# Plain fp32 q, k and v, with two heads in the row halves of TensorE, in the scoring and attention of a two-layer decoder step

## The chip, the cores and the metric

The kernel runs on one core of a Trainium2 chip, as one launch. The metric is the time of the launch on the device in microseconds (us). Times are of one execution each; three executions of the kernel before took 2971.18, 2973.40 and 2977.46 us.

TensorE (PE) multiplies, and its weight loads are shown as an engine of their own (PEld). VectorE (DVE), ScalarE (ACT) and GpSimd (POOL) work on SBUF, and DVE and ACT read PSUM, where PE writes. SyncE (SP) issues most DMAs. The engines run their own instruction lists and wait for each other on semaphores.

## The reference

A step of a decoder of two layers over a prompt of 1024 positions and a decode batch of 8 x 4 positions, all in float32. Layer 0 mixes by windowed means, layer 1 by sparse attention: a small indexer scores all keys of a query, the 256 best are kept, and softmax attention runs over those. Each is followed by a SwiGLU feed-forward layer. What matters here is the prompt's part of layer 1:

```python
def index_scores(qi, wi, ki):
    s = jnp.einsum('bthd,bsd->bths', qi, ki).astype(jnp.float32)      # 8 heads of 64
    return jnp.einsum('bths,bth->bts', jax.nn.relu(s), wi.astype(jnp.float32))

def block(args):                                   # 128 queries at a time
    qb, qib, wib, t0 = args
    tq = t0 + jnp.arange(Q_BLOCK)
    sc = index_scores(qib, wib, ki)
    sc = jnp.where((key_pos[None, :] <= tq[:, None])[None], sc, -jnp.inf)
    _, sel = lax.top_k(sc, n_sel)                  # n_sel = 256
    valid = sel <= tq[None, :, None]
    return sparse_attend(qb, k[b_idx, sel], v[b_idx, sel], valid)

def sparse_attend(q, k_sel, v_sel, valid):         # 16 heads of 64, 4 kv heads
    s = jnp.einsum('btngd,btknd->btngk', q, k_sel).astype(jnp.float32) * (HEAD_DIM ** -0.5)
    s = jnp.where(valid[:, :, None, None, :], s, -jnp.inf)
    p = jax.nn.softmax(s, axis=-1).astype(v_sel.dtype)
    return jnp.einsum('btngk,btknd->btngd', p, v_sel)
```

q, k, v, qi, ki and wi come out of one projection of the normed activations by a 1024 x 2120 matrix.

## The kernel before, in words

The program is a row of phases, each closed by a barrier of all engines: front (modulation, pooling mixer), feed-forward 0, projection, index, prompt attention, sample attention (the decode batch), output projection, feed-forward 1, final norm. The change touches the projection, the index phase, the prompt attention, and one source of a load in the sample attention.

**Split numbers.** A product in fp32r, a 4-byte format of fewer bits, is cheap for PE but rounded. So each fp32 operand is held as two fp32r parts, hi = round(x) (ACT copies it) and lo = x - hi (DVE or POOL subtracts), and products hi*hi, hi*lo and lo*hi are summed.

**Projection** (`projection_phase`). 17 tiles of 128 output columns by 3 chunks of 352 positions. For each, PE runs 24 matmuls (L940 to L942), then ACT rounds the sum to `shi` (L903) and DVE subtracts to `slo` (L958), and both go to DRAM (`halves`, L860 and L861). k, v and the last tile also go out as fp32 (L892, L864). The 32 sample positions are copied to `sq` and go out at the end (L865).

**Index** (`index_phase`). It loads v and the indexer's keys, turns v to position-major form on PE and splits it on DVE (L1187 and L1188). Then the blocks of 128 queries from the third to the eighth (i = 0 to 5, so 384 to 1024 keys) are scored. `qst` and `kst` hold hi in one half of the 128 rows and lo in the other, so one head with its 64 dimensions uses all rows, and two matmuls (L1121 with hi keys, L1122 with lo keys) give its scores for up to 512 keys. Heads alternate between two pairs of PSUM banks: PE may score head n once ACT has cleared head n-2. ACT applies relu (L1157), DVE multiplies by the head's weight and adds (L1204). Between blocks PE scores the samples (L1090, L1068), which are plain fp32. Then DVE searches the 256th best score of each query bit by bit (L1246, L1273), alone, and writes masks `mb`.

**Prompt attention** (`prompt_attention_phase`). 8 query blocks by 4 kv heads make 32 units of 4 heads each. A list written by hand, the same on each engine, sets the order by slots of one head: PE scores the next head (L1380, L1381, again hi and lo in row halves, two bank pairs in turn), DVE adds the mask and takes the maximum (L1427), ACT takes the exponential with its sum (L1489), DVE the reciprocal (L1440), POOL normalises (L1460). Two units later, each tile of 128 keys x 4 heads is turned by four PE transposes (L1391), copied to hi by ACT (L1494), its lo is made by DVE (L1432), and PE multiplies by v (L1402, L1403; `vst` holds hi and lo of v side by side as 128 output rows). At a unit's end ACT copies out the two halves (L1478, L1479) and POOL adds them (L1454). The outputs have two PSUM banks in turn.

## Time and profile before

| what | value |
|---|---|
| time, median of 3 (lowest, highest) | 2973.4 us (2971.18, 2977.46) |
| the profiled execution's own time | 2975.8 us |
| its span, first to last instruction | 2974.1 us |
| PE busy | 2432.2 us, 82% |
| DVE busy | 1432.9 us, 48% |
| ACT busy | 696.0 us, 23% |
| POOL busy | 775.6 us, 26% |
| mean granted TensorE clock | 0.906 of full speed |
| DMA | 230.76 MB, mean 78 GB/s |

The profiled execution's time is 2.4 us above the median, and 1.7 us above its span. Shares of busy time are means over phases with different limits, so the rows below are of single stretches of the span. Matmuls are pipelined: a row's duration of one matmul overlaps the next one's, and the distance between starts is what one costs in a stream. A plain fp32 matmul stands in the profile as two records, one after the other, on the same operands.

### The profile page before, as it was taken

The numbers are of one execution on the slowest core, as the hardware profiler recorded it, in microseconds if no ns is written. First come the engines' busy times: TensorE is split into PE (matmuls) and PEld (weight loads), VectorE is DVE, ScalarE is ACT, GpSimd is POOL, SyncE is SP. The second block draws the span as 40 slices with busy tenths as digits, with TensorE's granted clock in tenths as the row PEclk, the third lists the DMA queues.
The fourth block names the chain that finished last, engine by engine and source line by source line (L and its number), as shares of the span: only waits on it lengthen the run. The fifth ranks groups of instructions, "written<-read, shape, count | busy, mean of one in ns | idle before, by whom it ended". The sixth has DMA issues, their size and how long they took to land. (4 is left out here: it accounts for less than half of the span.)

```text
span 2974.1 us, 41911 instructions
## 1 busy us (share of the span) xinstructions
PE 2432.2 (82%) x15305; PEld 2232.2 (75%) x15305; DVE 1432.9 (48%) x3050; ACT 696.0 (23%) x1152; POOL 775.6 (26%) x594
## 2 busy tenths in 40 slices
PE   3649999999999499774303798797789999999995
PEld 2549999999999499543203576346679999999994
DVE  6663333333333710389996677343363333333336
ACT  2241111111110422230004888111231111111101
POOL 3432121112110355300002777312231112111210
PEclk8879999999999699887656999898889999999997
DMA  8521111111110344442201110751111111111101
GB/s 354 204 96 72 43 43 56 42 42 42 42 42 0 124 159 158 129 115 82 92 10 43 36 28 9 251 207 57 43 43 43 43 42 42 61 52 42 42 14 58
DMA packets 85773, 230.76 MB, mean 78 GB/s; under 512 B 14516, under 2 KB 50868, under 8 KB 71604
## 3 DMA queue, kind: packets, MB, share of 16 engines
q1 hardware_dynamic: 73264, 205.33, 19.8%
q0 software_dynamic: 10480, 23.85, 2.5%
q8 instruction: 55, 0.90, 0.1%
q10 hardware_dynamic: 1940, 0.40, 0.1%
q14 instruction: 34, 0.28, 0.0%
HBM read 200.77 MB, written 28.76 MB: 77 GB/s over the span
## 5 line engine op out<-in xcount | busy, mean ns | idle before, releaser
L740 PE MATMUL ps<-f_hhi,f_whi 128*128 128x352 f32 x2112 | 688.2, 326 | 30.4 <-DVE f_hlo L349 17.3
L741 PE MATMUL ps<-f_hhi,f_wlo 128*128 128x352 f32 x2112 | 682.8, 323 | 0.0
L742 PE MATMUL ps<-f_hlo,f_whi 128*128 128x352 f32 x2112 | 681.9, 323 | 0.0
L711 POOL TENSOR_TENSOR f_wlo<-f_raw,f_whi 128x2048 fp32r<-128x2048 f32 x66 | 303.9, 4605 | 1110.2 <-ACT f_whi L687 1110.2
L80 DVE SCALAR_TENSOR_TENSOR xT<-ps,mod,xT 128x352 f32<-128x352 f32 (+1 forms) x576 | 327.9, 572 | 212.6 <-PE ps L762 121.5
L740 PEld LDWEIGHTS ps<-f_hhi,f_whi 128*128 128x128 f32 x2112 | 401.3, 190 | 34.1 <-DVE f_hlo L349 34.1
L741 PEld LDWEIGHTS ps<-f_hhi,f_wlo 128*128 128x128 f32 x2112 | 401.9, 190 | 0.0
L742 PEld LDWEIGHTS ps<-f_hlo,f_whi 128*128 128x128 f32 x2112 | 400.8, 190 | 0.0
L760 PE MATMUL ps<-f_ahi,f_whi 128*128 128x352 f32 x1056 | 340.6, 323 | 0.0
L761 PE MATMUL ps<-f_ahi,f_wlo 128*128 128x352 f32 x1056 | 338.3, 320 | 0.0
L762 PE MATMUL ps<-f_alo,f_whi 128*128 128x352 f32 x1056 | 338.1, 320 | 0.0
L687 ACT ACTIVATE f_whi<-f_raw 128x2048 fp32r<-128x2048 f32 x66 | 126.4, 1915 | 553.4 <-PE ps L762 418.2
L1460 POOL TENSOR_TENSOR pa_pr<-pa_pr,pa_rl 128x128 f32<-128x128 f32 (+7 forms) x128 | 142.8, 1146 | 368.2 <-DVE pa_rl L1440 368.1
L780 DVE TENSOR_TENSOR f0n_g<-f0n_sq,ps 128x352 f32<-128x352 f32 x66 | 34.4, 521 | 399.7 <-PE ps L742 397.2
L780 DVE TENSOR_TENSOR f1n_g<-f1n_sq,ps 128x352 f32<-128x352 f32 x66 | 34.4, 521 | 399.0 <-PE ps L742 396.5
L761 PEld LDWEIGHTS ps<-f_ahi,f_wlo 128*128 128x128 f32 x1056 | 198.4, 188 | 0.0
L760 PEld LDWEIGHTS ps<-f_ahi,f_whi 128*128 128x128 f32 x1056 | 198.0, 188 | 0.0
L762 PEld LDWEIGHTS ps<-f_alo,f_whi 128*128 128x128 f32 x1056 | 197.9, 187 | 0.0
L940 PE MATMUL ps<-pj_hhi,pj_whi 128*128 128x352 f32 x408 | 135.0, 331 | 18.4 <-DVE pj_hlo L355 10.4
L1131 PE MATMUL ps<-ix_part,rowsum 128*128 128x1 f32 x64 | 16.3, 324 | 155.0 <-DVE ix_rel L1229 155.0
L1380 PE MATMUL ps<-kst,pa_qst 128*128 128x512 f32 (+3 forms) x192 | 74.7, 389 | 74.7 <-DMA pa_qst<-halves 41.3
L1432 DVE TENSOR_TENSOR pa_ptlo<-ps,pa_pthi 128x512 fp32r<-128x512 f32 x144 | 97.7, 689 | 78.8 <-ACT pa_pthi L1494 77.7
(323 smaller groups left out, 3902.5 us busy)
## 6 DMA issues: line engine op xcount, KB each, us to landing
f_raw<-in_ffn SPq DMA_DIRECT2D x66, 1024.0 KB, 4.7
ada_raw<-in_ada SPq DMA_DIRECT2D x18, 2048.0 KB, 12.0
sa_kv<-in_ckv POOLq DMA_DIRECT2D x54, 256.0 KB, 4.3
ix_vT<-in_ada SPq DMA_DIRECT2D x12, 1024.0 KB, 5.1
sa_kv<-in_ckv SPq DMA_DIRECT2D x42, 256.0 KB, 4.3
pj_raw<-in_win SPq DMA_DIRECT2D x9, 1024.0 KB, 5.7
pa_qst<-halves SPq DMA_DIRECT2D x128, 64.0 KB, 2.4
halves<-pj_shi SPq DMA_DIRECT2D x45, 176.0 KB, 1.8
```

Source lines behind the costliest of these rows:

```text
L80: ins = dve.scalar_tensor_tensor(out=x, in0=psum[:, 0:n], scalar=gate[:, 0:1], in1=x, op0=ALU.mult, op1=ALU.add)
L687: act.activation(whi[:, a, :], raw[:, a % 2, :], ACT.Copy).then_inc(w_hi, 1)
L711: pool.tensor_tensor(wlo[:, a, :], raw[:, a % 2, :], whi[:, a, :].bitcast(F32), ALU.subtract).then_inc(w_lo, 1)
L740: pe.matmul(c.ps[:, bank, 0:CH], hi[:, k, side, :], hhi[:, k, col], start=(k == 0), stop=False)
L741: pe.matmul(c.ps[:, bank, 0:CH], lo[:, k, side, :], hhi[:, k, col], start=False, stop=False)
L742: last = pe.matmul(c.ps[:, bank, 0:CH], hi[:, k, side, :], hlo[:, k, col], start=False, stop=(k == KD - 1))
L760: pe.matmul(c.ps[:, q % 6, 0:CH], hi[:, k, w], ahi[:, k, col], start=(k == 0), stop=False)
L761: pe.matmul(c.ps[:, q % 6, 0:CH], lo[:, k, w], ahi[:, k, col], start=False, stop=False)
L762: last = pe.matmul(c.ps[:, q % 6, 0:CH], hi[:, k, w], alo[:, k, col], start=False, stop=(k == 1))
L940: pe.matmul(c.ps[:, q, 0:CH], hi[:, k, w], hhi[:, k, col], start=(k == 0), stop=False)
L1432: dve.tensor_tensor(ptlo[:, t % 3, :], c.ps[:, 4 + t % 2, :], pthi[:, t % 3, :].bitcast(F32), ALU.subtract).then_inc(lo_ready, 1)
L1460: pool.tensor_tensor(p, p, rl[:, i % 3, g:g + 1].to_broadcast([P, (q + 1) * P]), ALU.mult).then_inc(p_ready, 1)
```

## The change

Everything that the prompt and the samples need of q, k and v is kept in plain fp32.

- Projection: ACT copies each chunk once to one of 6 fp32 buffers, and it goes out by one DMA, q to a new DRAM tensor `qf`. DVE has no part in it. `sq` and `halves` are gone.
- Index: v is copied by one DVE copy. `kst` holds the fp32 keys twice, in both row halves. `qst` holds head 2j in rows 0 to 63 and head 2j+1 in rows 64 to 127. One fp32 matmul of 64 rows gives one head's scores for up to 512 keys; the two heads' matmuls stand one after the other, on different row halves and banks. Before a pair PE waits until ACT has cleared all earlier heads.
- Prompt attention: 16 pairs of (query block, two kv heads), each of 4 slots of two heads. PE scores the two heads of the next slot once DVE has masked both heads of this one; there is one set of score banks. Each key tile is turned for two kv heads (8 transposes); ACT copies the turned tiles, and DVE the last one of a slot. Values of the two kv heads are two fp32 matmuls with 64 output rows each, to the two partition halves of one PSUM bank. The last key tile of a slot has its values a slot later. ACT and DVE each copy out one kv head's result; POOL adds nothing any more. Turning starts 5 slots after the scoring of a pair's first slot.
- The loads of q are one DMA where there were four; the sample attention reads `qf` in place of `sq`.

The order of the program's instructions in three places follows. A name in square brackets is a semaphore that the row waits for, by the name it was first allocated under: `pool_step` counts cleared heads of the index phase, `x_ready6` masked heads, `x_ready5` scored heads. A row with x3 is three more of the kind.

PE in the index phase, scores of the last query block (1024 keys), before, two heads:

```order
L1121 MATMUL ps<-ix_kst,ix_qst 128x512 [waits pool_step]
L1122 MATMUL ps<-ix_kst,ix_qst 128x512
L1121 MATMUL ps<-ix_kst,ix_qst 128x512
L1122 MATMUL ps<-ix_kst,ix_qst 128x512
L1121 MATMUL ps<-ix_kst,ix_qst 128x512 [waits pool_step]
L1122 MATMUL ps<-ix_kst,ix_qst 128x512
L1121 MATMUL ps<-ix_kst,ix_qst 128x512
L1122 MATMUL ps<-ix_kst,ix_qst 128x512
```

and now, two heads, the start of two more, and what follows the block:

```order
L1067 MATMUL ps<-ix_kst,ix_qst 128x512 [waits pool_step]
L1067 MATMUL ps<-ix_kst,ix_qst 128x512 x3
L1067 MATMUL ps<-ix_kst,ix_qst 128x512 [waits pool_step]
L1067 MATMUL ps<-ix_kst,ix_qst 128x512 x3
L1035 MATMUL ps<-xT,ix_qsb 32x512 [waits pool_s_diff]
L1035 MATMUL ps<-xT,ix_qsb 32x512 x3
```

Eight matmuls in fp32r with a wait before each head became four in plain fp32 with one wait before the pair.

PE in the prompt attention, last query block, before: a head's turn and values, the scores of the next head, and its two tiles.

```order
L1391 MATMUL ps<-ident,pa_pr 128x128 [waits silu_clear]
L1391 MATMUL ps<-ident,pa_pr 128x128 x3
L1402 MATMUL ps<-pa_pthi,vst 128x512 [waits silu_clear]
L1403 MATMUL ps<-pa_ptlo,vst 128x512
L1380 MATMUL ps<-kst,pa_qst 128x512 [waits x_ready6]
L1381 MATMUL ps<-kst,pa_qst 128x512
L1380 MATMUL ps<-kst,pa_qst 128x512
L1381 MATMUL ps<-kst,pa_qst 128x512
L1391 MATMUL ps<-ident,pa_pr 128x128 [waits silu_clear]
L1391 MATMUL ps<-ident,pa_pr 128x128 x3
L1402 MATMUL ps<-pa_pthi,vst 128x512 [waits silu_clear]
L1403 MATMUL ps<-pa_ptlo,vst 128x512
```

and now the scores of a slot (L1352), one key tile turned for two kv heads (L1368), the late values of the slot before (L1383), and the start of the second tile:

```order
L1352 MATMUL ps<-kst,pa_qst 128x512 [waits x_ready6,x_ready2]
L1352 MATMUL ps<-kst,pa_qst 128x512 x3
L1368 MATMUL ps<-ident,pa_pr 128x128 [waits small_ready]
L1368 MATMUL ps<-ident,pa_pr 128x128 x3
L1368 MATMUL ps<-ident,pa_pr 128x128 [waits small_ready]
L1368 MATMUL ps<-ident,pa_pr 128x128 x3
L1383 MATMUL ps<-pa_pt,vst 64x512 [waits silu_clear,small_ready]
L1383 MATMUL ps<-pa_pt,vst 64x512
L1368 MATMUL ps<-ident,pa_pr 128x128 [waits small_ready]
L1368 MATMUL ps<-ident,pa_pr 128x128 x3
```

All matmuls before used all 128 rows and all 128 columns of the array; now 64 rows x 128 columns, 128 x 128 and 128 x 64 follow each other.

DVE in the prompt attention, last query block, before:

```order
L1427 ISA pa_pr,pa_nb<-ps,mb 128x1024 [waits x_ready5]
L1427 ISA pa_nb 128x1
L1440 RECIPROCAL pa_rl<-pa_ls 128x4 [waits x_ready7]
L1432 TENSOR_TENSOR pa_ptlo<-ps,pa_pthi 128x512 [waits small_ready] x2
L1427 ISA pa_pr,pa_nb<-ps,mb 128x1024 [waits x_ready5]
L1427 ISA pa_nb 128x1
```

and now two heads masked, the copy, the reciprocal, the copy-out of a finished pair (with `quad_used`, which counts finished values), and the next two heads:

```order
L1425 ISA pa_pr,pa_nb<-ps,mb 128x1024 [waits x_ready5]
L1425 ISA pa_nb 128x1
L1425 ISA pa_pr,pa_nb<-ps,mb 128x1024 [waits x_ready5]
L1425 ISA pa_nb 128x1
L1431 COPY pa_pt<-ps 128x512 [waits quad_used,c_ready]
L1435 RECIPROCAL pa_rl<-pa_ls 128x2 [waits x_ready7]
L1437 COPY oT<-ps 64x2x128 [waits quad_used]
L1437 COPY oT<-ps 64x2x128
L1425 ISA pa_pr,pa_nb<-ps,mb 128x1024 [waits x_ready5,c_ready]
L1425 ISA pa_nb 128x1
```

The split of two tiles per head is gone, and once per pair (every fourth slot) a wait for PE's values stands between the masks of two slots.

The diff, cut to what the prediction speaks of:

```diff
-        shi, slo = sb("shi", [P, 3, CH], F32R), sb("slo", [P, 3, CH], F32R)
-        sf = sb("sf", [P, 3, CH])
-        sq = sb("sq", [P, 12, NS])
+        sf = sb("sf", [P, 6, CH])
...
-                        sp.dma_start(d.halves[split_tile(m), 0, :, col], shi[:, q, :].bitcast(F32)).then_inc(split_out[q], 16)
-                        sp.dma_start(d.halves[split_tile(m), 1, :, col], slo[:, q, :].bitcast(F32)).then_inc(split_out[q], 16)
-                    if f32_dst(m) is not None:
-                        q = (3 * n_f32.index(m) + ch) % 3
-                        sp.dma_start(f32_dst(m)[:, col], sf[:, q, :]).then_inc(f32_out[q], 16)
-            sp.dma_start(d.sq.rearrange("m p n -> p m n"), sq[:]).then_inc(sq_out, 16)
-            sp.wait_ge(sq_out, 16)
+                    n = 3 * m + ch
...
+                    sp.dma_start(f32_dst(m)[:, ch * CH:(ch + 1) * CH], sf[:, n % 6, :]).then_inc(f32_out[n % 6], 16)
...
+                sp.dma_start(qst[:, i % 2], d.qf[8:12, :, q * P:(q + 1) * P].rearrange("j p n -> p j n")).then_inc(q_ready[i % 2], 16)
...
-                for h in range(NIH):
+                for j in range(NIH // 2):
+                    n = NIH * i + 2 * j
                     if n >= 2:
-                        pe.wait_ge(r_ready, n - 1)
+                        pe.wait_ge(r_ready, n)
                     for k0 in range(0, L, 512):
                         w = min(512, L - k0)
-                        out = c.ps[:, 2 * (n % 2) + k0 // 512, 0:w]
-                        pe.matmul(out, qst[:, i % 2, h, :], kst[:, 0, k0:k0 + w], start=True, stop=False)
-                        last = pe.matmul(out, qst[:, i % 2, h, :], kst[:, 1, k0:k0 + w], start=False, stop=True)
-                    last.then_inc(s_ready, 1)
-                    n += 1
+                        for a in range(2):
+                            rows = slice(64 * a, 64 * a + 64)
+                            last = pe.matmul(c.ps[:, 2 * a + k0 // 512, 0:w], qst[rows, i % 2, j, :], kst[rows, k0:k0 + w], start=True, stop=True)
+                            if k0 + w == L:
+                                last.then_inc(s_ready, 1)
...
-                    link(dve.tensor_copy(c.vst[:, i, :, 0:HD], v))
-                    dve.tensor_tensor(c.vst[:, i, :, HD:P], v, c.vst[:, i, :, 0:HD].bitcast(F32), ALU.subtract)
+                    dve.tensor_copy(c.vst[:, i], v)
...
+        def share(s):
+            j, part = divmod(s - LAG, 4)
+            if not 0 <= j < NP:
+                return []
+            n = pairs[j][0] + 1
+            return [(j, kt) for kt in range(n * part // 4, n * (part + 1) // 4)]
...
-                if n >= 2:
-                    pe.wait_ge(m_ready, n - 1)
+                if sp == 0:
+                    pe.wait_ge(q_ready[i % 3], 16 * (i // 3 + 1))
+                if s:
+                    pe.wait_ge(m_ready, 2 * s)
                 for k0 in range(0, L, 512):
                     w = min(512, L - k0)
-                    out = c.ps[:, 2 * (n % 2) + k0 // 512, 0:w]
-                    pe.matmul(out, qst[:, i % 3, g, :], kst[:, v, 0, k0:k0 + w], start=True, stop=False)
-                    last = pe.matmul(out, qst[:, i % 3, g, :], kst[:, v, 1, k0:k0 + w], start=False, stop=True)
-                last.then_inc(s_ready, 1)
-
-            def turn(t):
-                i, kt = tiles[t]
+                    for a in range(2):
+                        rows = slice(64 * a, 64 * a + 64)
+                        last = pe.matmul(c.ps[:, 2 * a + k0 // 512, 0:w], qst[rows, i % 3, sp, :], kst[rows, 2 * vp + sp // 2, k0:k0 + w],
+                                         start=True, stop=True)
+                        if k0 + w == L:
+                            last.then_inc(s_ready, 1)
...
+            def values(j, kt):
...
+                if kt == 0 and j:
+                    pe.wait_ge(act_out, 2 * j)
+                    pe.wait_ge(dve_out, 2 * j)
...
+                for vl in range(2):
+                    last = pe.matmul(c.ps[64 * vl:64 * vl + 64, 7, :], c.vst[:, kt, 2 * vp + vl, :], place(j, kt, vl),
+                                     start=(kt == 0), stop=(kt == q))
+                last.then_inc(pv_done, 1)
+            scores(0)
+            for s in SLOTS:
+                if s + 1 < 4 * NP:
+                    scores(s + 1)
+                late = share(s - 1)[-1:] if s else []
+                todo = late + share(s)[:-1]
+                for j, kt in share(s):
+                    turn(j, kt)
+                    if todo:
+                        values(*todo.pop(0))
+                for j, kt in todo:
+                    values(j, kt)
...
+                    for a in range(2):
+                        dve.wait_ge(s_ready, 2 * s + a + 1)
...
+                for j, kt in share(s - 1)[-1:] if s else []:
+                    t = (j, kt, 1)
+                    dve.wait_ge(t_ready, turned[t] + 1)
+                    wait_place(dve, j, kt)
+                    dve.tensor_copy(place(*t), turn_bank(t)).then_inc(dve_copied, 1)
+                if 1 <= s <= 4 * NP:
+                    two = slice(2 * ((s - 1) % 2), 2 * ((s - 1) % 2) + 2)
+                    dve.wait_ge(e_ready, 2 * s)
+                    dve.reciprocal(rl[:, (s - 1) // 2 % 4, two], ls[:, (s - 1) // 2 % 4, two]).then_inc(rl_ready, 1)
+                for j in finished(s):
+                    read_output(dve, j, 1, lambda out, src: dve.tensor_copy(out, src), dve_out)
```

## Rows read from the trace of the kernel before

**Rows 1.** Busy us (and instructions) of PE, PEld, DVE, ACT, POOL; clock; DMA share, GB/s.

```profile
1240.10:1299.10 59.00, 55.72 (x272) 30.61 (x272) 44.10 (x52) 39.74 (x58) 7.33 (x16) 0.96 0.57 126
...
1587.00:1870.00 283.00, 228.00 (x1248) 175.81 (x1248) 186.84 (x432) 232.61 (x529) 190.00 (x193) 0.95 0.13 31
```

**Rows 2.** Timeline of the index phase at 1024 keys: start us, us, what [idle before].

```profile
1285.63 0.40 PE L1122 MATMUL ps<-ix_kst,ix_qst 128*128 128x512 f32 x1
...
1286.06 1.94 ACT L1157 ACTIVATE ix_rel<-ps 128x1024 f32<-128x1024 f32 x2 [1.47 <-PE ps L1122]
...
1287.14 0.50 PE L1121 MATMUL ps<-ix_kst,ix_qst 128*128 128x512 f32 x1 [0.20 <-ACT ix_rel L1157]
...
1287.48 0.40 PE L1122 MATMUL ps<-ix_kst,ix_qst 128*128 128x512 f32 x1
...
1287.72 0.40 PE L1121 MATMUL ps<-ix_kst,ix_qst 128*128 128x512 f32 x1
...
1289.47 0.50 PE L1121 MATMUL ps<-ix_kst,ix_qst 128*128 128x512 f32 x1 [0.20 <-ACT ix_rel L1157]
```

**Rows 3.** The five stretches in which PE scores prompt heads (columns of rows 1).

```profile
1240.10:1251.80 11.70, 10.62 (x33) 6.17 (x33) 8.65 (x17) 7.62 (x15) 4.16 (x9) 0.82 0.37 92
...
1254.60:1261.30 6.70, 6.37 (x34) 5.11 (x33) 4.46 (x7) 4.75 (x7) 0.29 (x1) 1.00 0.19 50
...
1265.20:1272.40 7.20, 6.59 (x33) 5.16 (x32) 4.78 (x6) 5.10 (x7) 0.00 (x0) 1.00 0.06 16
...
1273.60:1281.70 8.10, 7.52 (x34) 5.45 (x33) 7.25 (x8) 5.92 (x7) 0.60 (x1) 1.00 0.83 194
...
1284.80:1293.80 9.00, 8.40 (x33) 5.52 (x32) 6.63 (x7) 6.61 (x7) 0.29 (x1) 1.00 1.03 212
```

**Rows 4.** Prompt attention, query blocks 4 and 8 (columns of rows 1).

```profile
1654.50:1684.60 30.10, 23.86 (x126) 17.20 (x126) 19.56 (x51) 27.09 (x67) 20.98 (x25) 1.00 0.15 36
...
1798.40:1845.00 46.60, 42.34 (x239) 32.83 (x238) 38.30 (x67) 41.64 (x80) 33.95 (x24) 1.00 0.03 7
```

**Rows 5.** Groups by form, prompt attention: busy us, mean ns of one | idle before.

```profile
L1391 PE MATMUL ps<-ident,pa_pr 128*128 128x128 f32 x576 | 89.4, 278 | 11.9 <-DVE pa_ptlo L1432 8.4 <-POOL pa_pr L1460 3.2
L1494 ACT ACTIVATE pa_pthi<-ps 128x512 fp32r<-128x512 f32 x144 | 84.5, 596 | 31.5 <-PE ps L1391 29.3
...
L1427 DVE CUSTOM_DVE_ANT_0 pa_pr<-ps,mb 128x1024 f32<-128x1024 f32 x16 | 19.4, 1215 | 0.0
L1489 ACT ACTIVATE pa_pr<-pa_pr,pa_nb 128x1024 f32<-128x1024 f32 x16 | 18.4, 1149 | 0.2
...
L1427 DVE CUSTOM_DVE_ANT_0 pa_pr<-ps,mb 128x512 f32<-128x512 f32 x16 | 10.8, 681 | 0.0
```

**Rows 6.** Timeline: projection's end, v's turn, attention's first scores and last copy.

```profile
1213.71 0.46 ACT L892 ACTIVATE pj_sf<-ps 128x352 f32<-128x352 f32 x1 [2.80 <-PE ps L942]
...
1216.70 0.46 SPq L865 DMA_DIRECT2D sq<-pj_sq  x1
...
1232.15 0.42 DVE L1187 CAST vst<-ps 128x256 fp32r<-128x256 f32 x1 [16.86 <-PE ps L1109]
...
1591.76 0.47 PE L1380 MATMUL ps<-kst,pa_qst 128*128 128x128 f32 x1 [40.28 <-DMA pa_qst<-halves]
...
1867.71 0.38 ACT L1479 ACTIVATE pa_olo<-ps 64x256 f32<-64x256 f32 x1
```

**Rows 7.** Timeline of PE at the sample scores, plain fp32.

```profile
1261.30 1.06 PE L1090 MATMUL ps<-xT,ix_qsb 64*32 64x512 f32 x8
1262.29 1.05 PE L1068 MATMUL ps<-ix_rs,ix_ws 128*32 128x512 f32 x2
1263.27 1.06 PE L1090 MATMUL ps<-xT,ix_qsb 64*32 64x512 f32 x8
```

**Rows 8.** Group by form, index phase (columns of rows 5).

```profile
L1157 ACT ACTIVATE ix_rel<-ps 128x384 f32<-128x384 f32 x8 | 3.8, 491 | 27.9 <-PE ps L1122 27.6
```

**Rows 9.** Timeline, one tile's four transposes in the prompt attention.

```profile
1745.81 0.60 PE L1391 MATMUL ps<-ident,pa_pr 128*128 128x128 f32 x4
```

More of the change, by code:

```diff
@@ L1013, in _ @@
             for half in range(2):
-                for part_ in range(2):
-                    sp.dma_start(kst[64 * half:64 * half + 64, part_, :].bitcast(F32), d.halves[KITILE, part_, 0:64, 0:SEQ]).then_inc(stack_ready, 16)
+                sp.dma_start(kst[64 * half:64 * half + 64, :], d.kiwi[0:64, 0:SEQ]).then_inc(stack_ready, 16)
             for i, q in enumerate(BLK):
@@ L1326, in prompt_attention_phase @@
     G = NH // NKV
+    HALVES, PLACES, LAG = 5, 3, 5
     with ExitStack() as ctx:
@@ new lines, in prompt_attention_phase @@
+        NP = len(pairs)
+        SLOTS = range(4 * NP + LAG + 1)
+        pv0 = [sum(pairs[j][0] + 1 for j in range(i)) for i in range(NP + 1)]
+        def share(s):
[4 more added lines that the diff above has]
+            return [(j, kt) for kt in range(n * part // 4, n * (part + 1) // 4)]
+        act_tile, dve_tile, turned = {}, {}, {}
+        for s in SLOTS:
+            for j, kt in share(s):
+                for vl in range(2):
+                    t = (j, kt, vl)
+                    turned[t] = len(turned)
+                    if vl and (j, kt) == share(s)[-1]:
+                        dve_tile[t] = len(dve_tile)
+                    else:
+                        act_tile[t] = len(act_tile)
@@ L1394, in values @@
-            def values(t):
-                i, kt = tiles[t]
-                q, v = units[i]
-                if kt == 0 and i >= 2:
-                    pe.wait_ge(o_read, 2 * (i - 1))
-                pe.wait_ge(lo_ready, t + 1)
-                out = c.ps[:, 6 + i % 2, :]
-                pe.matmul(out, c.vst[:, kt, v, :], pthi[:, t % 3, :], start=(kt == 0), stop=False)
-                pe.matmul(out, c.vst[:, kt, v, :], ptlo[:, t % 3, :], start=False, stop=(kt == q)).then_inc(pv_done, 1)
-            scores(0, 0)
@@ L1406, in _ @@
-            for n in slots:
-                if n + 1 < NH_ALL:
-                    scores(*divmod(n + 1, G))
-                for t in share(n):
-                    turn(t)
-                    if t >= 2:
-                        values(t - 2)
-            values(len(tiles) - 2)
-            values(len(tiles) - 1)
+                    for a in range(2):
[4 more added lines that the diff above has]
+                            last.then_inc(s_ready, 1)
@@ new lines, in turn @@
+            def turn(j, kt):
+                if kt == 0:
+                    pe.wait_ge(p_ready, 2 * G * (j + 1))
+                for vl in range(2):
+                    t = (j, kt, vl)
+                    if t in dve_tile:
+                        if dve_tile[t] >= 1:
+                            pe.wait_ge(dve_copied, dve_tile[t])
+                    elif act_tile[t] >= 2:
+                        pe.wait_ge(act_copied, act_tile[t] - 1)
+                    for g in range(G):
+                        last = pe.transpose(turn_bank(t)[:, g * P:(g + 1) * P], probs(j, G * vl + g, kt * P, P), c.ident[:, :])
+                    last.then_inc(t_ready, 1)
@@ L1497, in _ @@
-            read_output(NU - 1)
+            for s in SLOTS:
+                i, sp = divmod(s, 4)
+                if s < 4 * NP:
+                    for a in range(2):
+                        p = probs(i, 2 * sp + a, 0, (pairs[i][0] + 1) * P)
+                        r = 2 * (s % 2) + a
+                        act.wait_ge(m_ready, 2 * s + a + 1)
+                        if a == 0 and s >= 8:
+                            act.wait_ge(rl_ready, s - 7)
+                        act.activation(p, p, ACT.Exp, bias=nb[:, s // 2 % 4, r:r + 1], scale=-1.0, accum_out=ls[:, s // 2 % 4, r:r + 1]).then_inc(e_ready, 1)
+                for j, kt in share(s):
+                    for vl in range(2):
+                        t = (j, kt, vl)
+                        if t in act_tile:
+                            act.wait_ge(t_ready, turned[t] + 1)
+                            wait_place(act, j, kt)
+                            act.activation(place(*t), turn_bank(t), ACT.Copy).then_inc(act_copied, 1)
+                for j in finished(s):
+                    read_output(act, j, 0, lambda out, src: act.activation(out, src, ACT.Copy), act_out)
```

265 lines of the change are left out of this document (90 added, 175 removed).

## The prediction

> **What bounds the kernel now.** I read the busy shares by phase first. The change touches three phases, and two have a length of their own that it can move: 59 us of index scoring and 283 us around the prompt attention [rows 1]; the search between them is not touched. The feed-forward phases and the projection are PE with fp32r weights, which stay.
>
> In the index scoring no engine is full: PE 55.7 of 59.0 us by its own rows, DVE 44.1, ACT 39.7 [rows 1]. The timeline at 1024 keys shows what sets the pace. PE scores two heads, waits until ACT has cleared the first, and starts again: 1287.14, then 1289.47, so 2.33 us for two heads. ACT begins its two relus at 1286.06 while PE is already in the second head, and they take 1.94 together [rows 2]. So scoring one head hides behind clearing another. The reader should see that this needs two sets of banks. The five stretches with prompt heads sum to 42.7 us [rows 3].
>
> In the attention the block windows show ACT first: 41.6 of 46.6 us at 1024 keys, 27.1 of 30.1 at 512, with PE at 42.3 and 23.9 [rows 4]; PE's records overlap each other's pipeline, so its busy time overstates how full it is, ACT's does not. By forms, a head at 1024 keys costs ACT 1.15 for the exponential, 2 x 0.60 for two tiles, and 4 x 0.38 per unit, 0.38 per head, for copies out: 2.73 of the 2.91 us that a head takes (46.6 over 16) [rows 4, 5, 6]. PE is close behind, so relieving ACT is worth only the distance to PE, a few tenths per head.
>
> **Price of a plain fp32 matmul.** The sample scores show it: eight records, four matmuls of 512 columns on both row halves and four column groups, run from 1261.30 to 1262.29, and the two records of a single matmul from 1262.29 to 1263.27, the same 0.98 to 0.99 [rows 7]. So one matmul is two passes of about 0.43 us per 512 columns, 2 columns' time each (512 at 2.4 GHz is 0.21), and neighbours on other parts of the array are free. What is left, 0.99 less 0.86, is 0.13 for loading weights that nothing hid and running empty before the array is cut another way. fp32r costs 0.23 to 0.24 per 512 columns (1287.48, 1287.72) [rows 2], and a head needed two. So a pair of heads per 512 keys costs 0.86 instead of 4 x 0.23 = 0.92, if the halves run together: PE's work in scores hardly changes.
>
> The first matmul after a wait also pays its 128 weight columns: 1287.14 to 1287.48 is 0.34 instead of 0.23, so 0.11 [rows 2].
>
> **Index phase.** Now PE waits before each pair for all heads before it, and both heads need both bank sets. So scoring and clearing follow each other. At 1024 keys: weights 0.11, 4 passes 1.72, from the last streaming to the relu 0.2 (matmul starts 1285.63, streams 0.23, relu at 1286.06), relus 1.94, back to PE 0.05: 4.02 per pair, against 2.33 [rows 2]. DVE's 44.1 us in the whole of it [rows 1] fit under the longer pace, so it does not bind. At 384 keys, with relus 491 ns each and 0.1 of overlap between two [rows 2, 8]: 0.11 + 0.64 + 0.2 + 0.88 + 0.05 = 1.88. The terms are linear in the keys, so the mean of the six blocks is 2.95 and 24 pairs take 70.8 us, 28 more than 42.7. The last pair of a block is cleared while PE scores samples, about 1 us in four or five places (-4); the first block runs at half clock (mean 0.82 in its stretch [rows 3]), with more of it on the path (+2). I take +26, bounds +15 (a third of the clearing hidden, DVE having set part of the old pace) and +35.
>
> **Attention.** I go slot by slot, two heads each. PE in a slot: scores S = 0.11 + 1.72 x keys/1024, then for each key tile a turn of 8 transposes, 0.11 apart (four take 0.60, of which the last is 0.28: three steps of 0.11) [rows 5, 9], so 0.87, and values of two kv heads on two column halves, one matmul's price, 0.86. All three cut the array differently: each segment pays the 0.1 of running empty, plus 0.11 of weights (0.05 for 64 columns). So a turn is 1.07 and values 1.01. Tiles per slot: (block number)/4.
> At 1024 keys a slot is 1.83 + 0.1 + 2 x 2.08 = 6.1, 3.05 per head where it was 2.91. At 512 keys 0.97 + 0.1 + 2.08 = 3.15, 1.58 per head against 1.88 (30.1 over 16) [rows 4].
> The masks of both heads must end before the next scores: 0.42 of hand-overs (0.22 from PE to DVE, 0.14 between the two, 0.06 back, estimates after the 0.2 and 0.05 of the relus) + 2 x 0.68 = 1.8 at 512, 0.42 + 2 x 1.215 = 2.85 at 1024 [rows 5], mostly under turning and values. But every fourth slot DVE's list has the copies out of the finished pair before the next masks, and they wait for values that PE issues after the next scores and one turn. Then values 0.91, 0.2 of latency, two reads at 0.42 (the 256-column cast [rows 6]), then the masks, are in a row: 0.1 + 1.07 + 0.91 + 0.2 + 0.9 + 0.2 + 2.43 = 5.8 instead of 4.3 after the scores at 1024 keys, 4.7 instead of 2.2 at 512 keys. Queued behind that wait are the masks, and behind them ACT's exponentials and PE's scores.
> Each slot is S plus the larger of PE's segments and the masks' row, and the fourth slots go by the long row. Summed over all slots by block of queries, with the first 12 slots at half clock: 13.8, 22.6, 22.8, 29.0, 32.9, 41.9, 48.0, 49.9, and 22.4 for the last turns and values: 283 us. Before it was 1591.76 to 1868.1, 276 [rows 6]; short blocks win up to 3, long ones lose up to 5. So +7. If drained switches and exposed weights cost nothing it is 253 (-24); if they cost twice and passes 0.44, 306 (+30).
> ACT: at 1024 keys 2 x 1.18 + 3 x 0.60 + 0.19 = 4.35 per slot, under PE's 6.1. POOL's sums (64 of 0.7) vanish from an engine that was not late.
>
> **The rest.** Projection: PE's list is the same and its clock is full, so ACT's and DVE's relief is nothing there (PE's stream hides it); SP issues 51 DMAs of q, k, v where it issued 105, with no queue behind them before. Its end loses the rounding, the subtraction and a row of DMAs between ACT at 1213.71 and the last issue at 1216.70: about 2.7 earlier [rows 6]. v's subtraction, 9 times 0.4 partly under transposes, gives 1.2; fewer DMA issues before the attention's first scores 0.7. Together -4.6, bounds -7 and -1.
>
> **Sum.** 2975.8 (the profiled time) + 26 + 7 - 4.6 = 3004. That execution stood 2.4 above the median, so 3002 for a median.
>
> **What the skill says.** The Trainium skill, "TensorEngine Tiling (Array Packing)", Key Properties, says that changing the tiling mode, not just the tile, drains TensorE. The trace agrees in kind, with the 0.13 around a sample segment [rows 7]; with it the attention is 283, without 253. The Trainium skill, "TensorE: Matmul & The Clock Gate", Part 3, says that matmuls on different row groups run concurrently, started a few ns apart; the rows show it only where column groups differ as well, and by its failing I would have the second rival.
>
> **Rivals.**
> (1) *PE gapless, slower no more.* Switches and weights cost nothing, and the copies out hide: attention is 221 by the same sum, -56; with index +26 the time is 2941, and with only one of the two (253 or 249) about 2971. It decides where a long slot takes under 5.6 us. For: the fp32 passes are slightly cheaper than fp32r, ACT's load falls by a quarter. Against: the 0.13 seen, and the order on DVE. Faster side: 7 in 100 below 2967, 7 in 100 at 2967 to 2979.
> (2) *Row halves with the same 128 columns do not run together.* Then all prompt scores double: +65 in the attention, +30 in the index, 3097. For: the only rows with two row halves have four column groups too. Against: nothing shows a queue there. 7 in 100.
> (3) *The clock falls in the index phase.* PE would be busy 1.8 of 4 us in a pair instead of nearly always. At 1.2 GHz the passes double, +31: 3033. For: the mean clock of the first stretch is 0.82, so the phase starts low [rows 3], and PE now pauses after every pair. Against: in the later stretches it is 1.00 with PE waiting once per two heads. 10 in 100.
> (4) *No change*: the long blocks' loss and the index are there by construction, so I give this nothing beyond (1).
>
> The likeliest, both phases longer and the clock full, gets 69 in 100, with a range of its own of 2985 to 3020. A measurement of this kernel can tell about 0.2%, 6 us, from no change. So faster 0.07, within 0.07, slower 0.86. The range 2978 to 3042 leaves out rivals 1 (mostly) and 2.
>
> **What would show it.** Index: pairs of relus 4.0 us apart at 1024 keys, and the search starting some 22 us later after its earlier start. Attention: masks in pairs, 6.1 us apart at 1024 keys, with one gap of 7.6 per four; DVE's idle time ended by PE's values. fp32 records of the two row halves starting together, and 0.1 between segments. I am wrong if the pairs of relus overlap the scores, if the granted clock is 0.5 in the index scoring, or if the long slots take 5.6 us or less.

## The result, and the profile of the changed kernel

The changed kernel took 3012.32 us as the median of four executions (3008.24 to 3019.89), the kernel before 2975.43 (2971.18 to 2978.46). The ratio is 1.0136, with a 95% interval of 1.0118 to 1.0153: slower, by 37 us. On another chip the ratio was 1.0126 (1.0106 to 1.0147). The forecast was 3002 us, with a range of 2978 to 3042.

The profiled execution took 3009.22 us, its span 3007.6, against 2975.8 and 2974.1 before. Its 33.4 us more lie as follows, by the starts and ends of the instructions that open and close each stretch:

| stretch | before | changed | difference |
|---|---|---|---|
| launch to feed-forward 0's first matmul | 188.6 | 192.2 | +3.5 |
| to the projection's last matmul | 1025.1 | 1024.6 | -0.5 |
| to the first index scores | 26.5 | 22.1 | -4.3 |
| index scoring, to the last relu | 54.8 | 82.8 | +27.9 |
| to the attention's first scores | 296.8 | 297.3 | +0.5 |
| attention, to the end of the last copy out | 276.3 | 292.1 | +15.8 |
| to the sample attention's first scores on `sa_kv` | 21.5 | 21.6 | +0.1 |
| sample attention | 131.8 | 122.3 | -9.5 |
| to the last instruction of DVE (3.6 us before the span's end) | 949.1 | 948.9 | -0.2 |

Two stretches of this list that the change doesn't touch, launch and sample attention, come back below.

**The two phases as a whole.** Windows over the index scoring and the attention of the changed kernel, with the columns of rows 1:

```profile
1238.85:1321.70 82.85, 54.41 (x250) 17.51 (x252) 43.05 (x53) 37.29 (x56) 6.96 (x15) 0.90 0.23 58
1619.00:1911.10 292.10, 246.76 (x1248) 120.22 (x1248) 144.71 (x404) 164.97 (x380) 144.14 (x128) 0.90 0.05 13
```

Against [rows 1] ACT's work in the attention fell from 233 to 165 us and DVE's from 187 to 145, as the split numbers went, and the phase is longer all the same. No engine is full in either row: what sets the pace is who waits for whom. The granted clock (TensorE's, a share of full speed) is 0.90 in both rows, where it was 0.96 and 0.95.

**Index scoring.** Timeline at 1024 keys; it answers to [rows 2]:

```profile
1309.68 1.99 PE L1067 MATMUL ps<-ix_kst,ix_qst 64*128 64x512 f32 x8 [2.02 <-ACT ix_rel L1102]
...
1311.70 1.94 ACT L1102 ACTIVATE ix_rel<-ps 128x1024 f32<-128x1024 f32 x2 [2.07 <-PE ps L1067]
...
1313.69 1.99 PE L1067 MATMUL ps<-ix_kst,ix_qst 64*128 64x512 f32 x8 [2.02 <-ACT ix_rel L1102]
```

PE works for 2 us and stands for 2 us, and ACT does the same in the other halves: 4.01 us per pair of heads, where it was 2.33. At 384 keys the pairs start 1.87 us apart:

```profile
1240.77 0.92 PE L1067 MATMUL ps<-ix_kst,ix_qst 64*128 64x384 f32 x4 [0.95 <-ACT ix_rel L1102]
```

The eight records at 1024 keys (two heads, two pieces of 512 keys, two passes) take 1.99, so the heads do run together: at 0.43 for a pass of 512 keys, one head after the other would need 3.4.

**An ordinary slot of the attention.** PE's timeline in the 8th block of queries:

```profile
1858.41 1.99 PE L1352 MATMUL ps<-kst,pa_qst 64*128 64x512 f32 x8
1860.33 1.09 PE L1368 MATMUL ps<-ident,pa_pr 128*128 128x128 f32 x8
1861.35 1.08 PE L1383 MATMUL ps<-pa_pt,vst 128*64 128x512 f32 x4
...
1864.39 1.99 PE L1352 MATMUL ps<-kst,pa_qst 64*128 64x512 f32 x8
```

From start to start, the scores take 1.92 us, a turn 1.02, and values 1.01 (the second turn, left out here, starts at 1862.36), the slot 5.98. None of these records carries a wait.

**A slot with copies out.** PE's timeline just ahead of that (in brackets the idle time before, and what ended it):

```profile
1843.37 1.99 PE L1352 MATMUL ps<-kst,pa_qst 64*128 64x512 f32 x8
...
1846.32 1.08 PE L1383 MATMUL ps<-pa_pt,vst 128*64 128x512 f32 x4
1850.79 2.77 PE L1352 MATMUL ps<-kst,pa_qst 64*128 64x512 f32 x8 [3.40 <-DVE pa_nb L1425]
1853.49 1.95 PE L1368 MATMUL ps<-ident,pa_pr 128*128 128x128 f32 x8
```

and DVE's:

```profile
1847.44 0.89 DVE L1437 COPY oT<-ps 64x256 f32<-64x256 f32 x2 [4.21 <-PE ps L1383]
1848.36 1.23 DVE L1425 CUSTOM_DVE_ANT_0 pa_pr<-ps,mb 128x1024 f32<-128x1024 f32 x1
```

The scores were ready before 1845.4, and the masks that need them start at 1848.36: DVE stood 4.21 us in front of the copies out, which wait for the values of 1846.32. PE then stands for 3.40. That was foreseen; what follows was not: the next scores take 2.77 us instead of 1.99 and the eight transposes 1.95 instead of 1.09. Windows over the stretch give the reason (the figure after POOL is the granted clock):

```profile
1847.50:1850.80 3.30, 0.01 (x1) 0.01 (x2) 3.24 (x7) 1.87 (x5) 0.00 (x0) 1.00 0.00 0
1851.90:1855.20 3.30, 3.30 (x14) 1.65 (x10) 1.62 (x3) 0.68 (x3) 3.30 (x2) 0.50 0.00 0
1855.30:1858.50 3.20, 3.20 (x19) 1.34 (x18) 1.42 (x4) 2.03 (x3) 0.15 (x1) 1.00 0.02 5
```

PE stood still in the first window, at full clock. A microsecond after it started again the granted clock was 0.50, TensorE's 1.2 GHz, and 3.4 us later it was 2.4 GHz again. In the blocks from the third on this comes with eight of the eleven waits of 2 us and over, the seven of 2.60 to 3.40 all among them. Before the change the clock was 1.00 in [rows 4]. The Trainium skill, "TensorE: Matmul & The Clock Gate", Part 1, section "HAM oscillation — how this bites in real kernels", describes the like for a kernel that waits for a DMA once in each tile: each wait sends the clock back to the half rate, and the next tile pays for it. The trace agrees, with shorter waits, for masks. My prediction had half clock in the first 12 slots of the attention and had not looked for it behind these waits.

The waits in the attention, summed (engine, line, what it waited for: us, times, longest):

```profile
DVE oT L1437 <- PE ps L1383: 44.4, 16, 4.2
PE ps L1352 <- DVE pa_nb L1425: 42.4, 31, 3.4
```

DVE stood for 44 us in front of the sixteen copies out, one per pair. PE's waits for masks sum to 42; thirteen of them are over 1.7 us and make 33 of it.

Blocks 4 and 8 of the attention, to set against [rows 4]:

```profile
1675.30:1704.60 29.30, 24.64 (x122) 11.01 (x122) 17.08 (x51) 17.15 (x43) 16.27 (x18) 0.94 0.07 19
1833.50:1882.20 48.70, 44.01 (x228) 20.60 (x228) 25.89 (x50) 29.35 (x53) 26.92 (x15) 0.96 0.00 1
```

### The profile page after: what moved, and what is told of

Its sections match the earlier page's. It is cut to its first block and busy times, and to the rows that moved or that the text cites. A ratio compares the mean times of both kernels' runs of the same rounds, so it can differ in the third digit from the quotient of the medians.

```text
span 3007.6 us, 41230 instructions
## 1 busy us (share of the span) xinstructions
PE 2447.0 (81%) x15305; PEld 2164.0 (72%) x15305; DVE 1364.8 (45%) x2969; ACT 621.9 (21%) x983; POOL 728.9 (24%) x530
## 5 line engine op out<-in xcount | busy, mean ns | idle before, releaser
L1352 PE MATMUL ps<-kst,pa_qst 64*128 64x512 f32 (+3 forms) x384 | 91.0, 584 | 82.7 <-DVE pa_nb L1425 42.4
L1352 PEld LDWEIGHTS ps<-kst,pa_qst 64*128 64x128 f32 x384 | 36.2, 212 | 143.8 <-DVE pa_nb L1425 67.7
```

The costliest lines, as they stand in the source:

```text
L1352: last = pe.matmul(c.ps[:, 2 * a + k0 // 512, 0:w], qst[rows, i % 3, sp, :], kst[rows, 2 * vp + sp // 2, k0:k0 + w], start=True, stop=True)
```

## Experiments

Two theories stood after the comparison. **A**: the index phase grew because a pair's scoring and clearing follow each other. **C**: the attention grew because DVE's copies out stand ahead of the next masks; PE's waits cost their own length, and the half clock behind them costs more. The rivals are in the texts of the expectations. Each ratio is to the kernel before on the same chip.

### Index scored in chunks that alternate between bank sets

```diff
-                L = (q + 1) * P
                 for j in range(NIH // 2):
-                    n = NIH * i + 2 * j
-                    if n >= 2:
-                        pe.wait_ge(r_ready, n)
-                    for k0 in range(0, L, 512):
-                        w = min(512, L - k0)
+                    for k0, w in chunks((q + 1) * P):
+                        if n >= 2:
+                            pe.wait_ge(r_ready, 2 * (n - 1))
                         for a in range(2):
                             rows = slice(64 * a, 64 * a + 64)
...
+                            pe.matmul(c.ps[:, 2 * (n % 2) + a, 0:w], qst[rows, i % 2, j, :], kst[rows, k0:k0 + w], start=True, stop=True).then_inc(s_ready, 1)
+                        n += 1
```

`chunks` gives one chunk up to 512 keys, else two. ACT clears chunk by chunk, and DVE waits for a head's last chunk. (In the code shown, lines with three dots stand for lines left out.)

> The index phase alone is changed: a pair of heads is scored and cleared in two chunks of keys (one chunk up to 512 keys), and the chunks use the two sets of banks in turn, so that PE can score the next chunk while ACT clears the last. The arithmetic and the plain fp32 row halves stay. Theory A (the index phase grew by 28 us because scoring and clearing of a pair follow each other): pairs of relus fall from 4.0 to about 2.3 us apart at 1024 keys (four relus of 128x512 of about 0.59, which overlap by 0.1) and from 1.88 to about 1.1 at 384; first relu to last relu falls from 81.8 to 55 to 60 us; the time is 22 to 26 us less than the changed kernel, about 2988. Rival B (the plain fp32 passes or the half clock made it longer): the pairs at 1024 keys stay above 3.4 us apart and the time is at most 8 us less.

Measured: 2979.15 us, ratio 1.0037 (1.0019 to 1.0055), against 1.0136 and 1.0126 of the changed kernel: 26 to 29 us less. The window over the scoring, from the first scores to the last relu, then PE's timeline at 1024 keys:

```profile
1237.50:1292.35 54.85, 48.36 (x245) 14.82 (x244) 42.02 (x52) 40.45 (x88) 6.96 (x15) 1.00 0.35 89
```

```profile
1281.53 1.99 PE L1074 MATMUL ps<-ix_kst,ix_qst 64*128 64x512 f32 x8
1283.82 2.11 PE L1074 MATMUL ps<-ix_kst,ix_qst 64*128 64x512 f32 x8 [0.31 <-ACT ix_rel L1110]
1286.12 2.11 PE L1074 MATMUL ps<-ix_kst,ix_qst 64*128 64x512 f32 x8 [0.19 <-ACT ix_rel L1110]
```

The pace is 2.29 to 2.30 us per pair (2.33 in the kernel before), with the same fp32 matmuls: theory A is shown, and rival B falls. The phase lost 28 us and is as long as before the change, 54.8; the time lost 26 to 29 where 22 to 26 was expected. Some of that is clock. With PE busy it was 1.00; in the changed kernel it was 0.76 and 0.63 in the first two of these windows:

```profile
1248.00:1262.00 14.00, 10.17 (x38) 2.60 (x38) 5.86 (x8) 5.87 (x12) 2.56 (x5) 0.76 0.10 29
1262.00:1276.00 14.00, 10.62 (x42) 3.59 (x42) 6.74 (x8) 5.06 (x8) 0.29 (x1) 0.63 0.08 20
1276.00:1321.70 45.70, 28.78 (x152) 9.79 (x152) 24.59 (x23) 22.47 (x29) 0.59 (x2) 1.00 0.32 81
```

Pairs of the changed kernel with the same work, 640 keys, the first at full clock:

```profile
1262.62 1.35 PE L1067 MATMUL ps<-ix_kst,ix_qst 64*128 64x512 f32 x8 [1.38 <-ACT ix_rel L1102]
1265.35 2.50 PE L1067 MATMUL ps<-ix_kst,ix_qst 64*128 64x512 f32 x8 [1.38 <-ACT ix_rel L1102]
1269.23 2.50 PE L1067 MATMUL ps<-ix_kst,ix_qst 64*128 64x512 f32 x8 [1.38 <-ACT ix_rel L1102]
```

From start to start the first pair takes 2.73 us, the second, at half clock, 3.88. Four pairs ran so, two in this block and two at 512 keys, where a pair took 3.19 instead of 2.30. That is some 4 us of the 28, an estimate from these figures.

### The copies out taken from DVE, or put behind the masks

In the first kernel ACT does the copies of both kv heads; in the second DVE keeps its own, one place later.

```diff
-                for j in finished(s):
-                    read_output(dve, j, 1, lambda out, src: dve.tensor_copy(out, src), dve_out)
 ...
-                    read_output(act, j, 0, ...)
+                    for vl in range(2):
+                        read_output(act, j, vl, ...)
```

> In the attention ACT does the copies out of both kv heads; DVE no longer waits for the values. Theory C (in every fourth slot the masks stand behind copies out that wait for values; PE then stands still for 1.8 to 3.4 us, and the granted clock falls to 0.5 for 3.4 us after the gap): the sixteen gaps (33 us together) go, the slot at 1024 keys that took 9.0 us takes 6.0 to 6.5, the granted clock from the third block on is 1.00, and attention takes 250 to 262 us where it took 292; the time is 30 to 41 us less, 2971 to 2982. Rival D (the low clock comes without regard to the gaps, and the masks are late for another reason): the granted clock still falls to 0.5 about once per pair, and the time is 0 to 15 us less.

```diff
                     for a in range(2):
                         dve.wait_ge(s_ready, 2 * s + a + 1)
 ...                                                       # the two masks
+                for j in finished(s - 1) if s else []:
+                    read_output(dve, j, 1, ...)
                 for j, kt in share(s - 1)[-1:] if s else []:
 ...
-                for j in finished(s):
-                    read_output(dve, j, 1, ...)
```

> DVE keeps its copies out, but they stand behind the masks of the next slot instead of ahead of them. Theory C: the masks come in time, and only the values of the next pair's first tile wait for the copies (about 0.5 us at 1024 keys); the time is 25 to 40 us less than the changed kernel, close to the kernel in which ACT does all copies out. Rival E (what counts is DVE's or ACT's load, not the place of the copies in the list): the load is the same, so the time is the same within 6 us.

Measured: 2972.98 us, ratio 1.0009 (0.9992 to 1.0026), and 2970.53 us, ratio 0.9997 (0.9983 to 1.0011). The attention of the first, then of the second:

```profile
1619.30:1868.40 249.10, 228.92 (x1248) 111.00 (x1248) 131.49 (x372) 175.61 (x412) 144.04 (x128) 0.96 0.06 15
```

```profile
1622.20:1867.30 245.10, 229.11 (x1248) 111.09 (x1248) 144.91 (x404) 163.16 (x380) 143.99 (x128) 0.96 0.06 15
```

292 us became 249 and 245. In the second kernel DVE has the load of the changed kernel (144.9 us for 144.7), so it was the place of two instructions, and rival E falls. The low stretches went with the waits: from 1637.5 us on in the first kernel, and from 1640.3 in the second, the clock is 1.00 to the phase's end. Rival D falls too. In the second kernel the masks at a pair's end start behind their scores (the second follows at 1830.30), the copies out come after them, and PE's one wait in this place is for ACT's copies:

```profile
1829.15 1.23 DVE L1425 CUSTOM_DVE_ANT_0 pa_pr<-ps,mb 128x1024 f32<-128x1024 f32 x1 [2.27 <-PE ps L1352]
...
1831.56 0.89 DVE L1428 COPY oT<-ps 64x256 f32<-64x256 f32 x2
...
1832.98 1.08 PE L1383 MATMUL ps<-pa_pt,vst 128*64 128x512 f32 x4 [0.91 <-ACT oT L1472]
```

The phase gained 43 and 47 us, the time only 35 to 41 us by the ratios. In both profiles the sample attention takes 131 us, as before the change, where the changed kernel's profile had 122, and the index scoring, whose code is that of the changed kernel, 86.0 us where it had 82.8; more of that below. (The text expected sixteen gaps of 33 us together; the 33 us are in thirteen.)

### PE kept busy in the gaps

```diff
                 if s + 1 < 4 * NP:
+                    if any(kt == pairs[j][0] for j, kt in share(s - 2)) and pairs[s // 4][0] >= 3:
+                        gap = 1.2 + 2 * (0.15 + 0.00104 * P * (pairs[s // 4][0] + 1)) - (1.0 if len(share(s - 1)) > 1 else 0.0)
+                        free = sum(len(share(r)) * 2 - bool(share(r)) for r in range(s))
+                        pe.wait_ge(act_copied, free - 1)
+                        for _ in range(int(0.8 * gap / 0.11)):
+                            pe.transpose(c.ps[:, 4 + free % 2, 0:P], c.ident[:, :], c.ident[:, :])
                     scores(s + 1)
```

> The changed kernel with 10 to 24 extra transposes of the identity (128 columns, 0.11 us each) into a free bank, on PE in most of the gaps ahead of the late scores; they take 80 in 100 of each gap and compute nothing that is used. Only PE gets more to do. Theory C: the gap stays for the masks, but PE does not stand still in it, the granted clock stays 1.00 behind it, and each of the 10 long slots loses 1 to 1.5 us: the time is 8 to 15 us less than the changed kernel. Rival D (the clock falls without regard to the gaps): the low stretches stay and the time is 0 to 5 us more.

Measured: 3007.21 us, ratio 1.0123 (1.0089 to 1.0156), with an attention of 280.1 us. The phase gained what theory C said; the interval of the time holds both theories. The next two runs stand side by side on one chip.

> The changed kernel as it is, timed beside the others on the same chip. It should stand at 1.012 to 1.015 of the kernel before. Its profile is a second sample of the clock: the low stretches behind the gaps in the attention should be there again (theory C), and the sample attention takes 122 or 132 us, by the clock it happens to get.

> The kernel with extra transposes in PE's gaps again, with more rounds and on the same chip as the changed kernel. Theory C: attention 278 to 282 us against 292, and 8 to 15 us less in the time than the changed kernel. Rival D: the attention phase gains as in the first look, but the time does not, because the clock is lower elsewhere: 0 to 4 us less.

Measured: the changed kernel 3008.50 us, ratio 1.0126 (1.0106 to 1.0147); with the extra transposes 3005.77, ratio 1.0111 (1.0093 to 1.0129). Of the changed kernel's second profile, attention and sample attention:

```profile
1616.60:1908.60 292.00, 246.69 (x1248) 120.25 (x1248) 144.67 (x404) 164.96 (x380) 144.13 (x128) 0.90 0.05 13
1930.30:2055.00 124.70, 116.97 (x588) 56.85 (x587) 53.27 (x119) 18.38 (x32) 28.63 (x50) 0.95 0.65 220
```

and of the filled kernel: attention, the blocks from the third on in it (to the last mask), sample attention:

```profile
1619.00:1900.30 281.30, 258.45 (x1461) 136.31 (x1461) 144.30 (x404) 164.55 (x380) 144.01 (x128) 0.95 0.05 13
...
1655.60:1871.40 215.80, 205.99 (x1205) 109.09 (x1202) 122.38 (x305) 131.61 (x282) 122.50 (x95) 1.00 0.05 12
...
1921.40:2052.80 131.40, 123.58 (x588) 60.20 (x587) 53.43 (x119) 18.37 (x32) 28.09 (x50) 0.90 0.62 211
```

And one gap of it:

```profile
1836.41 3.06 PE L1395 MATMUL ps<-ident 128*128 128x128 f32 x26
1839.88 1.99 PE L1352 MATMUL ps<-kst,pa_qst 64*128 64x512 f32 x8 [0.41 <-DVE pa_nb L1431]
1841.80 1.09 PE L1368 MATMUL ps<-ident,pa_pr 128*128 128x128 f32 x8
```

With 213 transposes more on PE the attention is 11 to 12 us shorter, in both profiles of this kernel. The masks are as late as ever, but behind the filled gap scores take 1.99 us and transposes 1.09: in these blocks PE's standing still is what brings the clock down, and that alone costs 11 us of the phase. In the time the gain was 2.7 us with overlapping intervals, so the 8 to 15 us that theory C gave the whole kernel are not seen and rival D's 0 to 4 is. The two profiles of these runs show where it went: the filled kernel had 6.6 us more in the sample attention (131.4 for 124.8) and 2.5 more in the index scoring (85.1 for 82.6), both with the same instructions and at a lower clock. The first profile of the filled kernel had 122.5 and 82.8 us there, so neither phase is the same in two executions of one kernel. Why the clock was lower there is open; that the filled gaps have a part in it is not shown and not ruled out.

### Both heads on the same row half

This kernel was built on the version with both gains, which comes next. The second head of each slot is scored from the first head's rows, so it computes another head's scores.

```diff
                     for a in range(2):
-                        rows = slice(64 * a, 64 * a + 64)
+                        rows = slice(0, 64)
                         last = pe.matmul(c.ps[:, 2 * a + k0 // 512, 0:w], qst[rows, i % 3, sp, :], ...)
```

> The kernel with both gains, but in the attention the second head of each slot is scored with the row half, and so the query, of the first head: both heads' fp32 matmuls stand on rows 0 to 63 (the second head's scores are thus another head's). The number of matmuls is the same. Theory G (two fp32 matmuls on different row halves run together, with 128 columns each, and a slot pays for one): on the same rows they follow each other, a slot at 1024 keys grows by 1.7 us and the attention by 50 to 62 us. Rival H (the row halves share nothing, the pace comes from elsewhere): the attention stays within 5 us of 245.

Measured: 3017.25 us, ratio 1.0155 (1.0127 to 1.0182), two executions. PE's timeline at 1024 keys, then windows over blocks 1 to 3 and the rest of the attention:

```profile
1857.21 3.70 PE L1360 MATMUL ps<-kst,pa_qst 64*128 64x512 f32 x8
1860.84 1.09 PE L1376 MATMUL ps<-ident,pa_pr 128*128 128x128 f32 x8
```

```profile
1587.80:1668.50 80.70, 75.68 (x179) 39.96 (x180) 31.12 (x135) 33.35 (x111) 26.46 (x46) 0.50 0.08 20
1668.50:1916.30 247.80, 245.05 (x1070) 118.33 (x1068) 117.64 (x270) 131.64 (x269) 117.50 (x83) 0.99 0.03 8
```

The same windows of the version it was built on:

```profile
1588.90:1635.50 46.60, 36.04 (x182) 18.03 (x183) 28.78 (x135) 32.09 (x111) 25.78 (x45) 0.81 0.13 35
1635.50:1833.90 198.40, 192.95 (x1068) 92.96 (x1067) 116.08 (x270) 130.98 (x270) 118.06 (x84) 1.00 0.04 10
```

The scores of a slot take 3.63 us instead of 1.92, so 1.71 more, and blocks 4 to 8 take 49.4 us more, where 1.72 x 8 x (4+5+6+7+8)/8 gives 51.6. Theory G is shown: on different row halves two fp32 matmuls with 128 columns each are paid as one. The Trainium skill, "TensorE: Matmul & The Clock Gate", Part 3, says that tiles on different row groups overlap, with an example of 32 rows; the runs agree for two halves of 64 rows with all columns. The first three blocks grew by 34 us instead of 10, which no text expected: there the granted clock stayed 0.50 for the whole window, with PE busy 76 of 81 us, where it had averaged 0.81. So the attention as a whole grew by 83 us, not by 50 to 62. Why the clock came back so late is open.

### Both gains together

The kernel has the index in chunks and DVE's copies out behind the masks, with no other edit.

> The index phase in two chunks of keys and DVE's copies out behind the next masks, together. Theories A and C act in different phases, so the gains add: index phase 54 us from first to last relu, attention 245, and the time is 28 to 29 us less than the kernel with late copies alone, about 2942, which is 0.990 to 0.992 of the kernel before. Rival F (the sample attention or the search gives part of it back by a lower clock, as it gave 9 us back in the run with ACT's copies): the time is 2948 to 2955.

Measured: 2940.56 us (2936.00 to 2944.08), ratio 0.9899 (0.9882 to 0.9917): faster than both kernels, by 30 us and by 68. Index scoring (first scores to last relu), attention and sample attention:

```profile
1236.00:1290.80 54.80, 48.30 (x245) 14.81 (x244) 42.09 (x53) 40.40 (x88) 6.81 (x15) 1.00 0.35 88
1588.90:1833.90 245.00, 228.99 (x1248) 110.99 (x1248) 144.86 (x404) 163.07 (x380) 143.84 (x128) 0.96 0.06 15
1856.70:1982.50 125.80, 117.13 (x588) 56.95 (x587) 53.29 (x119) 18.37 (x32) 27.67 (x49) 0.95 0.63 215
```

The two gains add; rival F falls.

## Why the prediction was right, and which terms were off

**Sign and causes held.** Both phases became longer by the two waits that were named. The time is 10 us above the forecast and inside the range, but less closely than that looks. By phase I expected +26, +7 and -4.6; the profile shows +27.9, +15.8 and -4.3, which is 39 and not 28. Two stretches that the change does not touch gave 6 back in this execution (-9.5 and +3.5). That was luck.

**Index, predicted +26, measured +27.9.** Pairs predicted 4.02 and 1.88 us apart came 4.01 apart at 1024 keys (1309.68 to 1313.69) and 1.87 at 384. I had put the half clock at 2 us in the first block; that block ran at full clock, and the second and third were low in part (0.76 and 0.63 above), at some 4 us. So this term was too small and in the wrong place. Rival 3 was half right there: the clock did fall with PE waiting in each pair, but from 1276 on it was 1.00, although PE had work for only 29 of 46 us.

**Attention, predicted +7, measured +15.8.** The terms, by the experiments, in us of the phase:

| term | predicted | shown by | measured |
|---|---|---|---|
| attention with no long slot | 249 | copies behind the masks | 245 |
| the long slots | +34 | filled gaps less that | +36 |
| half clock behind them | 0 | changed kernel less filled gaps | +11 |
| sum | 283 | | 292 |

The slot was predicted at 6.1 and is 5.98: scores 1.92 for 1.93, turn 1.02 for 1.07, values 1.01 for 1.01, so the sum of passes, weights and the 0.1 for cutting the array anew was read rightly from [rows 7]. The pass is also measured by itself (1.71 us for four passes, 0.43 each, on one row half); no run takes the 0.1 apart from the weights. A fourth slot was to take 7.6 from scores to scores, and took 7.42 (1843.37 to 1850.79). The step that failed is the one that made the next slot an ordinary one: "with the first 12 slots at half clock", and all others full. It took 7.62 us (1850.79 to 1858.41) instead of 5.98. I had worked out gaps of some 3 us for PE and had put the clock behind them at nothing. The block sums also had errors that offset each other: the tail behind the last mask took 28.9 us for 22.4, at full clock, and the blocks without their waits less than I gave them. The filled gaps leave a fifth of each gap open and the first blocks as they were, and the two profiles of that kernel differ by 1.3 us, so the 36 and the 11 are good to an us or two. They are us of the phase: in the time of the whole kernel the 11 did not show.

**The rest, predicted -4.6.** From the projection's last matmul to the first index scores it is 4.3 less, where -2.7 and -1.2 were forecast for it (the subtraction of v stands 8 times in the trace, not 9). The row at the end of the projection answers to [rows 6]: ACT's last copy at 1216.79 is followed by the last issue at 1217.28, 0.5 later where it was 3.0.

```profile
1216.79 0.46 ACT L865 ACTIVATE pj_sf<-ps 128x352 f32<-128x352 f32 x1 [3.35 <-PE ps L902]
```

```profile
1217.28 0.32 SPq L844 DMA_DIRECT2D kiwi<-pj_sf  x1
```

The 0.7 at the attention's start isn't to be seen: that stretch is 0.5 longer. No run took the projection's part alone; the 4.3 rests on the comparison of traces, but the same stretch is between 20.0 and 22.2 us in all nine profiles of a kernel with the new projection.

**Rivals.** (1), the cheap PE, was right about what the change can do and wrong about the order in which it stood: without the waits the attention is 31 us shorter than before the change. That switches and weights cost nothing, its other half, did not come: the slot is 5.98 us long, as with them. (2) was refuted by the kernel on one row half, where a slot's scores cost 1.71 us more. (3) came in part, in the second and third block of the index scoring. (4), no change, did not come.

## What to carry to other kernels

A row of instructions in one engine's list is a promise about order: put what frees a buffer behind what the next stage waits for, unless the buffer is needed sooner. When two outputs are produced together, they also have to be drained together, and a scheme that was double-buffered becomes serial without a line that says so; cut the work so that the two halves of the banks alternate. Price a gap on PE as its length plus what the half clock takes from the work behind it, here 36 and 11 us of the phase. Judge such a kernel by phases as well as by its time: the clock of phases that were not touched can hide a gain, or lend one.

## What the runs showed of the hardware that I had not expected

- Waits of PE of 2.60 to 3.40 us in the attention came with a fall of the granted clock to 0.50 seven times of seven, one of 2.33 us once of two, waits of 2.06 us in neither of two, and this was the same in the changed kernel's second profile. Length alone does not decide it: both waits of 1.8 us in the second block came with a fall too, and in the first profile of the filled kernel one of 2.06 did. From the third block on, six of the eight falls in the changed kernel's first profile lay 0.6 to 1.2 us behind PE's restart and two 0.1 to 0.4 us ahead of it.
- PE doing work for nothing (213 transposes, 25.4 us of records) made its phase 11 us shorter, and the time 2.7, which is not clear of noise.
- The sample attention, with the same instructions, comes in steps: 122 us in four profiles with one stretch at 0.50 in it, 125 to 126 in two with three such stretches, 131 to 132 in four with seven. One kernel gave 122.5 and 131.4, another 122.3 and 124.8. The launch until the first feed-forward matmul varied from 188.6 to 192.2 us, and the index scoring of the changed kernel's code from 82.6 to 86.0, by how much of it ran at 0.50. The first two together can move a time by 13 us, where 37 were to be explained.
- Two plain fp32 matmuls of 64 rows, 128 columns and 512 moving columns on different row halves take 0.43 us per pass together, and 0.86 on the same half (1.71 us more for the four passes of a slot at 1024 keys).
